# Recurrence and chunkwise memory layer: projections in another order, gate inputs with tokens in partitions, rows turned undivided

## The reference

```python
z = h @ w_in + b_in                       # 1024 -> 3080 columns
x_rg, g_rg, q, k, v, o, i_pre, f_pre = jnp.split(z, cuts, axis=-1)   # 6 x 512, 2 x 4
xc = causal_dwconv(x_rg, rg_conv_w, rg_conv_b)                        # 4 taps
y_rg = rg_lru(xc, ...) * jax.nn.gelu(g_rg, approximate=True)
qk = jax.nn.silu(causal_dwconv(jnp.concatenate([q, k], axis=-1), ml_conv_w, ml_conv_b))
hm = mlstm_chunkwise(q, k, v, i_pre, f_pre)       # per head
hm = rms_norm_2(hm, ml_norm)                      # over the 128 of a head
y_ml = jax.nn.sigmoid(o) * hm
return jnp.concatenate([y_rg, y_ml], axis=-1) @ w_out

# rg_lru: r, i = sigmoid(block matmuls of xc); a = exp(-8 r softplus(-lam))
#         u = sqrt(1 - a^2) * (i * xc);  h_t = a_t h_{t-1} + u_t
# mlstm:  log_f = log_sigmoid(f_pre); b = cumsum(log_f); weights
#         exp(b_t - b_s + i_s - m_t) for s <= t, times q.k, summed over v,
#         divided by max(|sum of weights|, exp(-m_t))
```

## Time and profile before

| | us |
|---|---|
| median of 3 runs | 2296.62 (2296.34 to 2297.12) |
| profiled execution | 2295.38 |
| its span, first to last instruction | 2293.6 |
| TensorE, VectorE, ScalarE busy in the span | 2163.3, 1793.0, 1373.8 |
| the layer's stretch from the first matmul on hy_w to the norm's spread | 148.7 (1524.0 to 1672.7) |

### The profile page before, as it was taken

How to read it: one execution, slowest core, us unless ns; L and a number is a source line. 1 busy time by engine, 2 the same in 40 slices (tenths; PEclk the granted TensorE clock), 3 DMA queues, 4 the chain that set the end, 5 groups by cost and what they waited for, 6 DMA issues and landing times.

```text
span 2293.6 us, 30853 instructions
## 1 busy us (share of the span) xinstructions
PE 2163.3 (94%) x12416; PEld 1896.2 (83%) x12416; DVE 1793.0 (78%) x2362; ACT 1373.8 (60%) x1787; POOL 45.1 (2%) x22
## 2 busy tenths in 40 slices
PE   7989999979999999999999999856799998999998
PEld 6989989868888888888888888746689997889997
DVE  4776666759898999999999989758667767768766
ACT  4544445558777777877787777544444445454443
POOL 0020002010000000000000000010000000000000
PEclk9999999979999999999999999978899999999999
DMA  8446644629999999999999999443236554326553
GB/s 272 138 130 201 204 145 156 217 100 384 350 367 362 360 363 351 366 346 367 341 374 350 360 347 363 182 130 110 78 125 216 175 183 140 118 92 203 184 172 109
DMA packets 280166, 546.64 MB, mean 238 GB/s; under 512 B 8524, under 2 KB 113616, under 8 KB 279888
## 3 DMA queue, kind: packets, MB, share of 16 engines
q1 hardware_dynamic: 276800, 535.33, 66.7%
q10 hardware_dynamic: 3040, 8.72, 1.0%
q0 software_dynamic: 176, 0.53, 0.1%
HBM read 543.49 MB, written 1.05 MB: 237 GB/s over the span
## 4 chain that ended last, share of the span: by engine, by line
PE 88%; DVE 8%; ACT 2%; DMA 1%; issue 1%; DVEq 0%; SPq 0%; ACTq 0%
PE psum L408 19%; PE psum L410 19%; PE psum L409 18%; PE psum L402 8%; PE psum L403 8%; PE psum L404 8%; DVE wl L391 2%; PE psum L1763 1%; PE psum L1783 1%; DMA raw<-in_w_in 1%; PE psum L1773 1%; DVE arena L2217 0%; PE psum L924 0%; PE psum L2473 0%; DVE SC L504 0%
## 5 line engine op out<-in xcount | busy, mean ns | idle before, releaser
L391 DVE TENSOR_TENSOR wl<-raw,wh 128x1024 fp32r<-128x1024 f32 x640 | 769.2, 1229 | 182.0 <-ACT wh L383 176.8
L383 ACT ACTIVATE wh<-raw 128x1024 fp32r<-128x1024 f32 x640 | 659.4, 1050 | 274.4 <-PE psum L404 132.6
L402 PE MATMUL psum<-xh,wh 128*128 128x256 f32 x1600 | 462.2, 289 | 23.8 <-DVE wl L391 18.7
L391 DVE TENSOR_TENSOR wl<-arena,wh 128x1024 fp32r<-128x1024 f32 x384 | 458.0, 1221 | 32.3 <-ACT wh L383 23.8
L408 PE MATMUL psum<-wh,xh 128*128 128x512 f32 (+1 forms) x1152 | 457.9, 397 | 18.7 <-DVE xl L428 10.4
L383 ACT ACTIVATE wh<-arena 128x1024 fp32r<-128x1024 f32 x384 | 404.6, 1062 | 94.3 <-PE psum L410 94.2
L403 PE MATMUL psum<-xl,wh 128*128 128x256 f32 x1600 | 458.2, 286 | 0.0
L404 PE MATMUL psum<-xh,wl 128*128 128x256 f32 x1600 | 457.7, 286 | 0.0
L410 PE MATMUL psum<-wh,xl 128*128 128x512 f32 (+1 forms) x1152 | 450.7, 391 | 0.0
L409 PE MATMUL psum<-wl,xh 128*128 128x512 f32 (+1 forms) x1152 | 450.5, 391 | 0.0
L402 PEld LDWEIGHTS psum<-xh,wh 128*128 128x128 f32 x1600 | 312.6, 195 | 30.4 <-DVE wl L391 14.6
(11 more groups left out here) (370 smaller groups left out, 1660.5 us busy)
## 6 DMA issues: line engine op xcount, KB each, us to landing
arena<-in_moe_g SPq DMA_DIRECT2D x72, 1024.0 KB, 7.3
arena<-in_moe_u SPq DMA_DIRECT2D x72, 1024.0 KB, 7.8
raw<-in_moe_d SPq DMA_DIRECT2D x64, 1024.0 KB, 7.4
arena<-in_moe_d SPq DMA_DIRECT2D x48, 1024.0 KB, 6.9
raw<-in_ff_up SPq DMA_DIRECT2D x48, 1024.0 KB, 5.2
raw<-in_moe_g SPq DMA_DIRECT2D x40, 1024.0 KB, 7.5
raw<-in_moe_u SPq DMA_DIRECT2D x40, 1024.0 KB, 7.3
raw<-in_ff_down SPq DMA_DIRECT2D x24, 1024.0 KB, 4.9
```

The costliest lines, as they stand in the source:

```text
L383: A.activation(unit(s, i)[0], raw_half(s, i), ACT.Copy).then_inc(*s.w_hi.tick(i))
L391: V.tensor_tensor(lo, raw_half(s, i), hi.bitcast(F), SUB).then_inc(*s.w_lo.tick(i))
L402: T.matmul(ps, wh, x[0][:, k, :], start=k == 0, stop=False)
```

## The change

- The order of loads and projections is xr, q, k, gr, v, oo; it was q, k, xr, v, gr, oo. The gate products of the recurrence follow q.
- The gate inputs are computed as 128 tokens x 8 per half (the tokens as the stationary side, `wif` moving; the bias by one more matmul with `DIF`). The log sigmoid runs on 128 x 2 x 4; `gate_rows` turns the result into rows of 4 x 256, on which only the scans run.
- The weights are turned by transposes, undivided. The divisor is not applied: its square, times 1e-6, takes the place of the norm's epsilon (`divisors`, `DD`), since the norm that follows cancels any factor of a row.
- The tiles of the two query halves are apart (`HL[t]`, `HP[t]`). Both row spreads and both products of q and k stand together, and so do both products with v.
- The recurrence's half of the output is split into `YH`, `YL`, so `pe_project` reads `YY` for its first four chunks.
- All four chunks of a projection leave PSUM on ScalarE. Factors that VectorE applied (softplus of lambda, 0.044715 in gelu, the norm's gain, half the bias of oo) are scale and bias of ScalarE's operations. The silus run two chunks at a time.
- ScalarE copies the two vectors of the next norms ahead of the first high part of the layer.
- `diags`, `pe_pT`, `dve_pT`, `act_pT`, `pe_av` and `act_av` are gone.

```diff
-            for name, c in (("q", 1024), ("k", 1536), ("xr", 0)):
+            for name, c in (("xr", 0), ("q", 1024), ("k", 1536), ("gr", 512)):
...
-        proj(0, "q", xw=by_chunks("nm0"))
-        ps, wif = claim(1), S("wif").rearrange("p (k n) -> p k n", k=8)
-        for m in range(2):
-            for k in range(8):
-                x = T.matmul(ps[0:4, m * 256:(m + 1) * 256], wif[:, k, 4 * m:4 * m + 4], XT[:, k, :], start=k == 0, stop=k == 7)
...
+            for t in range(2):
+                o = ps[:, t * 8:(t + 1) * 8]
+                for k in range(8):
+                    T.matmul(o, XT[:, k, t * P:(t + 1) * P], wif[:, k, :], start=k == 0, stop=False)
+                x = T.matmul(o, ones[0:4, :], DIF, start=False, stop=True)
...
+        proj(0, "xr", xw=by_chunks("nm0"))
+        gate_inputs()
+        proj(2, "q")
+        gates()
+        gate_rows()
+        proj(2, "k", (None, None, rows_turned, spread_rows))
+        proj(3, "gr")
...
+                if (n, h) == (0, 0):
+                    logits()
+        drained(1, (dve, "hy.v"))
+        turn(0, 3)
+        turn(1, 2)
+        proj(0, "oo", (weigh,))
+        sums()
+        pe_project("hy", (1, 3), lambda kk: YY if kk < 4 else XX, halves("hyo"), {2: norm},
...
         act_vector("nf0", 2, GAIN["nf0"])
         act_vector("np0", 3, GAIN["np0"])
+        hi_to(main, u0 + 2)
         hi_to(main, u0 + 4)
+        conv(0, "xr", XC, XR, 0, rw, S("rcb"), 0)
...
+        for f, dst in ((ACT.Exp, AA), (ACT.Tanh, TR)):
+            for c in range(4):
+                A.activation(dst[:, c, :], TR[:, c, :], f, scale=NSP[:, c:c + 1], bias=NSP[:, c:c + 1]
+                             ).then_inc(*act.tick("hy.ta"))
...
+            V.tensor_scalar(DN, DN, 1e18, 1e-3, MIN, MUL).then_inc(*dve.tick())
+            V.wait_ge(*dve.last())
+            V.tensor_tensor(DD, DN, DN, MUL).then_inc(*dve.tick("hy.dd"))
...
+        taps(XC[:, 0, :], XR[:, 0, :], rw, 0, "hy.xc")
+        V.wait_ge(*pe.of("hy.if"))
+        V.tensor_copy(IFS, pair(1)[:, 0:16].rearrange("p (t n) -> p t n", t=2)).then_inc(*dve.tick("hy.ifs"))
+        V.wait_ge(*dve.last())
+        dve_min_abs(IFW, IFS[:, :, 4:8])
...
+        V.tensor_tensor(HV, pair(1).rearrange("p (t n) -> p t n", t=2), BV[:, :].unsqueeze(1).to_broadcast([P, 2, 512]), ADD
                         ).then_inc(*dve.tick("hy.v"))
+        V.wait_ge(*pe.of("hy.T1"))
+        V.tensor_copy(HP[1][:, 0:2, :], heads(pair(2), 4)[:, 0:2, :]).then_inc(*dve.tick("hy.p1"))
+        divisors()
...
+        dve_scales("hy.ss", 2, 4, 1.0 / 128, DD)
```

More of the change, by code:

```diff
@@ L194, in all_loads @@
                 w.add(f"hy.v{n}", block(x, 512 * n, 2048, 512), (4, 512), "rows")
[L195 to L197 removed]
+            for n in range(2):
+                w.add(f"hy.oo{n}", cols(x, 2560 + 256 * n, 256), (8, 256))
         else:
@@ new lines, in weigh @@
+        def weigh():
+            ps = claim(3)
+            T.wait_ge(*dve.of("hy.v"))
+            for t in range(2):
+                T.wait_ge(*act.of(f"hy.p{t}"))
+                if t:
+                    T.wait_ge(*dve.of("hy.p1"))
+                for h in range(4):
+                    for kb in range(t + 1):
+                        x = T.matmul(ps[:, t * 512 + h * P:t * 512 + (h + 1) * P], HV[:, kb, h * P:(h + 1) * P],
+                                     HP[t][:, h, kb * P:(kb + 1) * P], start=kb == 0, stop=kb == t)
+                x.then_inc(*pe.tick(f"hy.av{t}"))
+                empties(6 + t, (act, f"hy.mt{t}"))
@@ new lines, in sums, with norm @@
+        def sums():
+            T.wait_ge(*act.of("hy.sq"))
+            pe_sums("hy.ss", 2, [[AA[:, h, :]] for h in range(4)], False)
+        def norm():
+            T.wait_ge(*dve.of("hy.ss.r"))
+            ps = claim(2)
+            for h in range(4):
+                x = spread(ps[:, h * 256:(h + 1) * 256], scales_at(4), h, 1)
+            x.then_inc(*pe.tick("hy.sp"))
+            drained(2, (dve, "hy.mrg"))
+        proj(0, "xr", xw=by_chunks("nm0"))
+        gate_inputs()
+        proj(2, "q")
@@ new lines, in act_hybrid @@
+        A.wait_ge(*act.of("hy.mt1"))
+        A.wait_ge(*dve.of("hy.aa"))
+        A.activation(AA, MT[:, 4:8, :], ACT.Square).then_inc(*act.tick("hy.sq"))
+        A.wait_ge(*pe.of("hy.oo"))
+        for c in range(4):
+            A.activation(OO[:, c, :], pair(0)[:, c * 256:(c + 1) * 256], ACT.Tanh, scale=0.5, bias=HBO[:, c:c + 1]
+                         ).then_inc(*act.tick("hy.oo"))
+        A.wait_ge(*act.last())
+        for c in range(4):
+            A.activation(OO[:, c, :], OO[:, c, :], ACT.Identity, scale=HMN[:, c:c + 1], bias=HMN[:, c:c + 1]
+                         ).then_inc(*act.tick("hy.og"))
@@ L2328, in dve_hybrid @@
[L2328 to L2337 removed]
+        weigh_in(0)
```

469 lines of the change are left out of this document (190 added, 279 removed).

## The result

| | before | after |
|---|---|---|
| median of the runs of one comparison | 2296.87 (4 runs, 2296.34 to 2300.28) | 2259.60 (4 runs, 2254.34 to 2264.67) |
| profiled execution, its span | 2295.38, 2293.6 | 2258.59, 2256.8 |

The ratio is 0.9834, with a 95% interval of 0.981 to 0.9859. Predicted were 2258, within 2250 to 2268.

A forecast was written before the change was run, and what follows sets the result against it. TensorE, busy 94% of the span, was taken as the bound, idle 34.9 us in the rewritten stage. Gains of 47.1 us less costs of 8.6 gave 38.5 net, so 2258 us, range 2250 to 2268.

The forecast's parts named there:

- (a): TensorE's wait ahead of v for the gate sums, 16.6 us, goes through smaller 128 x 8 steps and the new order.
- (b): Waits for the diagonals of the divisors, 4.5 + 2.0 us, go because the rows are turned undivided.
- (c): Wait for the recurrence's output parts, 10.4 us, goes: recurrence computed before v, its half split early into YH, YL.
- (d): TensorE work: narrow gate inputs save 2.9 us, transposes replacing the diagonals' product 1.4 more; gate-row transposes add 0.6.
- (e): Layer's start: ScalarE's gain-vector copies, now ahead of the first high part, delay the first matmul by 1.9 us.
- (f): At the row spread TensorE waits until VectorE has taken the turned rows out of their bank: 1.7 us added.
- (g): Ahead of the product with v TensorE waits for VectorE: 1.7 us added.
- (h): Clock behind the narrow gate-input block: costs from nothing to 5.3 us, taken as 1.7.
- (i): Clock falls behind the waits at row spread and product with v: each may cost 1.6 us; half counted, 1.6.
- rival 1: ScalarE becomes late; waits at row spread and product with v grow about 4 us each; 2266 to 2270 us; chance 0.17.
- rival 2: Added waits at row spread and product with v do not come and the clock holds; 2251 us; chance 0.14.
- rival 3: Gate sums are late again, TensorE stands some 10 us before k; 2270 us; chance 0.08.

The follow-up runs named there:

- rows_old: Changed kernel's projection order with the gate inputs and log sigmoid in the old four-row format; 2270.36 us, against 2259.11 for the changed kernel beside it.
- tok_old_order: Kernel before, order kept, with only the gate inputs changed to tokens in partitions and turned into rows for the scans; 2288.72 us, ratio 0.9964.
- divided: Changed kernel with the recurrence's weights divided again ahead of their turning, on VectorE instead of by diagonals on TensorE; 2263.14 us.
- three_moves: Changed kernel with operations on VectorE and ScalarE reordered to remove the three new waits of 1.8, 1.0 and 2.0 us; 2254.24 us.
- split_b: Second run of split_narrow without an edit, timed beside the changed kernel; 2249.35 us, against 2260.69 for the changed kernel.
- split_narrow: three_moves with the narrow gate-input block cut in two, 9 of its 18 matmuls moved behind q's first unit; 2250.93 us.
- vec_back: Changed kernel with the first units' high parts put back ahead of ScalarE's copies of gain vectors; 2259.80 us.
- xx_back: Changed kernel with the recurrence's half of the output split where the kernel before splits it, without YH and YL; 2258.17 us.

## Why the prediction was right, point by point

**The waits (a), (b), (c).** Right in whole: 34.9 us are gone. The placing on the old times held closely. Ready and asked, in the changed kernel's trace: gate rows 1553.8 and 1557.0 (3.2 to spare, 2.9 predicted); row sums 1561.6 and 1566.2 (4.6; 4.5); k 1584.9 and 1589.3 (4.4; 2.4); weighed rows 1593.8 and 1600.1 (6.3; 4.9); YL 1610.9 and 1619.6 (8.7; 8.6). Two of these times, from VectorE and TensorE in order of time:

```profile
1553.65 0.17 DVE L2269 SCALAR_TENSOR_TENSOR arena<-arena 128x8 f32<-128x8 f32 x1
```

```profile
1557.02 0.27 PE L1982 MATMUL psum<-consts,arena 128*4 128x128 f32 x1
```

The reason given for (a) was right: rows_old and tok_old_order show that order and smaller steps each take away more than half of the wait. For (b) the waits went, but the reason, that the diagonals go, is not what did it: divided, which divides in the new order, has no wait ahead of the turning either, so the order did it, and by an estimate from its rows would have with diagonals too. For (c) the reason was half right: the order did it, the tiles YH and YL did not.

**Work on TensorE (d).** The gate inputs took 4.35 us where I had 4.1 from L513's row; the 12 transposes took 1.47 where I had 1.7. TensorE in order of time at the gate inputs:

```profile
1535.94 1.85 PE L1973 MATMUL psum<-smalls,XT 128*128 128x8 f32 x16
1537.72 0.38 PE L1974 MATMUL psum<-SC,consts 4*128 4x8 f32 x2
1538.03 1.95 PE L1973 MATMUL psum<-smalls,XT 128*128 128x8 f32 x16
1539.91 0.38 PE L1974 MATMUL psum<-SC,consts 4*128 4x8 f32 x2
```

**The added waits (e), (f), (g).** 1.8, 1.0 and 2.0 us, against 1.9, 1.7 and 1.7. Each is where it was said, and three_moves removed all three by the edits that their reasons name.

**The clock (h), (i).** (h) was 1.7 us, as taken: 3.6 us at 0.53 behind the narrow block. (i) was counted as half of two stretches of 1.6 behind (f) and (g); one of 1.6 came, behind (f). The sum is right, which is luck, since its reason is wrong: three_moves has the stretch without the wait. Of the clock as a whole I had 8.5 - 1.7 - 1.6 = 5.2 us of gain; the layer's loss fell from 11.1 to 6.4, by 4.7.

**The sum.** 38.5 us were predicted for the layer and 39.6 came. The step that failed is the last one: "it arrives in full". Behind the layer 6.1 us were lost again (604.4 to 610.5), with the same instructions, by the clock (8.3 to 15.8 us lost). That the order behind the layer stays as it was did not keep its time. Had the part ahead of the layer not been 3.4 us shorter in the profiled execution, its time would have been some 2262. In the profiled execution these two partly cancel, and that it came so near the forecast is in part luck. The median of 2259.60 is 1.6 from the forecast; the other executions have no profile, so what makes it up is not shown.

**The signs.** The granted clock of 0.95 and no wait over 2.5 us inside the layer were right. The length of the stretch from the first matmul to the norm's spread was given as 109 to 112 us and is 107.3: the sum of 38.5 holds term (e), which lies ahead of that stretch, so that 148.7 - 38.5 - 1.9 = 108.3 was the number to give, and the net gain is 1.1 us larger besides.

**The rivals.** ScalarE late (rival 1): no, k had 4.4 us to spare. Waits that don't come (rival 2): they came. Gate sums late (rival 3): no, by 3.2 us. Clock at half (rival 4): not in the layer.

## What to carry to other kernels

Place the new order on the old trace, operation by operation, for both sides of every handoff: five spare times came out within 2 us, and four of the added costs within 0.7. Such sums are good for the waits, but they do not say which part of a change removes one: here one part that the prediction credited, the missing diagonals, was not needed for it. The clock has to be kept in a second account, since here removed waits were worth at least their length without the clock's share, and with it, in one profile each, three waits of 4.8 us were worth 3.1 and one of 1.8 nothing. A short run of narrow matmuls may be paid for in the wide matmuls behind it, and here so it was in 9 of 9 profiles; it is worth looking at the clock behind such a run before counting its saving.

## What the runs showed of the hardware that I had not expected

- Half clock behind a row spread (8 matmuls on weights of 4 partitions, 2.9 us at full clock) without any idle time of TensorE ahead of it: in three_moves 0.80 over the spread and 5.3 us at 0.50 behind it, in split_b 6.9 us at 0.52 from within the spread on, none in split_narrow, the same program as split_b.
- 16.5 us of the second stack's attention at 1.2 GHz in four of four profiles of the changed kernel, and as long in divided, rows_old and tok_old_order, where the kernel before and the other variants (vec_back, three_moves, split_narrow, split_b, xx_back) stand at half clock for some 7 us. It costs 5 to 6 us and differs between kernels whose layers are equally long (after and xx_back). What decides it stays open; all of them have the same instructions in the same order from the layer's end on, and no run here was made to move that place by a known time.
- Wait or no wait of 2.0 us ahead of the product with v, TensorE's clock stayed at 1.00 behind it (after, three_moves), whereas the same length of wait had half clock behind it in the kernel before. Behind the wait of 3.0 us there in divided it was 0.51 for 3.5 us.
